# Two latent units ahead of the dilated queries, a rotation that goes through PSUM, and three neighbourhood units behind the first scores

## The reference

```python
h = rms_norm(x, g_mix[l])
proj = h @ w_in[l]
c_q, c_kv, k_r, qkv_b, qkv_c, gate_logits = jnp.split(proj, IN_SPLITS, axis=-1)
y_a = mla_mixer(c_q, c_kv, k_r, ...)            # 8 heads, latents of rank 256 and 128
q_b = apply_rope(qkv_b[:, :, 0], cos_b, sin_b)   # 12 dilated heads of 64
k_b = apply_rope(qkv_b[:, :, 1], cos_b, sin_b)
y_b = dilated_mixer(q_b, k_b, qkv_b[:, :, 2])
y_c = neighbourhood_mixer(qkv_c[:, :, 0], qkv_c[:, :, 1], qkv_c[:, :, 2], rpb[l])   # 8 heads
x = x + (gates[:, :, 0] * (y_a @ w_pa[l]) + gates[:, :, 1] * (y_b @ w_pb[l])
         + gates[:, :, 2] * (y_c @ w_pc[l])) @ w_o[l]
x = x + (silu(rms_norm(x, g_ffn[l]) @ w1[l]) * (... @ w3[l])) @ w2[l]
```

## Time and profile before

| | |
|---|---|
| median of 3 runs | 2680.39 us (2680.01 to 2680.91) |
| the profiled execution | 2676.88 us, span 2675.1 us |
| mean granted TensorE clock | 0.974 of full speed |
| TensorE matmul | 2541.6 us busy, 95 % |
| TensorE weight load | 2085.9 us, 78 % |
| GpSimd | 1975.9 us, 74 % |
| VectorE | 1182.4 us, 44 % |
| ScalarE | 688.3 us, 26 % |
| DMA | 226.62 MB, mean 85 GB/s |

### The profile page before, as it was taken

One profiled execution on the slowest core, in us unless ns is written; L12 is line 12 of the kernel. 1 busy time (PEld: TensorE's weight loads), 2 busy tenths in 40 slices (PEclk: granted clock), 3 DMA queues, 4 the chain that ended last, 5 costly groups with the idle time before them and its releaser, 6 DMA issues.

```text
span 2675.1 us, 37616 instructions
## 1 busy us (share of the span) xinstructions
PE 2541.6 (95%) x12524; PEld 2085.9 (78%) x12524; DVE 1182.4 (44%) x1608; ACT 688.3 (26%) x1299; POOL 1975.9 (74%) x1576
## 2 busy tenths in 40 slices
PE   7999999999999999999999999999998899969997
PEld 5777878777788887778788877788886778848796
DVE  6846525224312125946615223422225237550774
ACT  4435214111201013535314111210002214131341
POOL 6976763889989888976862989999897573447704
PEclk9999999999999999999999999999998899969998
DMA  3222420232232222222421232232222121102201
GB/s 130 87 95 86 151 79 27 92 98 90 95 101 94 94 95 87 79 96 86 158 79 33 86 98 91 95 101 94 94 98 86 56 80 55 41 34 86 85 11 63
DMA packets 67572, 226.62 MB, mean 85 GB/s; under 512 B 7553, under 2 KB 16257, under 8 KB 66945
## 3 DMA queue, kind: packets, MB, share of 16 engines
q1 hardware_dynamic: 66736, 223.95, 25.0%
q10 hardware_dynamic: 720, 1.17, 0.1%
HBM read 222.99 MB, written 2.10 MB: 84 GB/s over the span
## 4 chain that ended last, share of the span: by engine, by line
POOL 48%; issue 34%; PE 8%; DMA 4%; DVE 3%; POOLq 2%; SPq 0%; DVEq 0%; ACT 0%
POOL whi L460 25%; POOL wlo L463 16%; POOL raw L479 3%; POOL ada_acc L481 2%; PE ps L555 2%; PE ps L556 2%; PE ps L557 2%; DMA raw<-w_gate 1%; DMA raw<-w_abc 1%; POOLq L462 1%; POOL lnsq L487 1%; DMA raw<-w 1%; DVE q_parts L1791 1%; POOLq L105 1%; POOLq L455 0%
## 5 line engine op out<-in xcount | busy, mean ns | idle before, releaser
L460 POOL TENSOR_TENSOR whi<-raw,one 128x512 fp32r<-128x512 f32 (+3 forms) x732 | 812.9, 1111 | 563.7 <-PE ps L557 480.8
L463 POOL TENSOR_TENSOR wlo<-raw,whi 128x512 fp32r<-128x512 f32 (+3 forms) x732 | 965.3, 1319 | 57.4
L555 PE MATMUL ps<-h,whi 128*128 128x512 f32 x1984 | 793.7, 400 | 46.1 <-POOL wlo L463 19.5
L556 PE MATMUL ps<-h,whi 128*128 128x512 f32 x1984 | 777.5, 392 | 0.0
L557 PE MATMUL ps<-h,wlo 128*128 128x512 f32 x1984 | 776.6, 391 | 0.0
L555 PEld LDWEIGHTS ps<-h,whi 128*128 128x128 f32 x1984 | 374.6, 189 | 148.0 <-POOL wlo L463 34.0
L557 PEld LDWEIGHTS ps<-h,wlo 128*128 128x128 f32 x1984 | 374.4, 189 | 81.2
L556 PEld LDWEIGHTS ps<-h,whi 128*128 128x128 f32 x1984 | 375.1, 189 | 78.0 <-issue 2.4
L555 PE MATMUL ps<-y,whi 128*128 128x512 f32 x640 | 250.0, 391 | 0.6 <-DVE y L1715 0.6
L557 PE MATMUL ps<-y,wlo 128*128 128x512 f32 x640 | 249.0, 389 | 0.0
L556 PE MATMUL ps<-y,whi 128*128 128x512 f32 x640 | 249.0, 389 | 0.0
(11 more groups left out here) (253 smaller groups left out, 3232.2 us busy)
## 6 DMA issues: line engine op xcount, KB each, us to landing
raw<-w SPq DMA_DIRECT2D x120, 512.0 KB, 3.2
raw<-w_abc SPq DMA_DIRECT2D x68, 512.0 KB, 3.2
raw<-w_ada SPq DMA_DIRECT2D x48, 512.0 KB, 3.3
raw<-w_gate SPq DMA_DIRECT2D x48, 512.0 KB, 3.3
raw<-w_in SPq DMA_DIRECT2D x44, 512.0 KB, 3.3
raw<-w_pac SPq DMA_DIRECT2D x16, 512.0 KB, 3.3
raw<-w_o SPq DMA_DIRECT2D x16, 512.0 KB, 3.2
raw<-w_out SPq DMA_DIRECT2D x16, 512.0 KB, 3.3
```

What stands on the lines that cost most here:

```text
L460: pool.tensor_tensor(whi[:, s, r], raw[:, s, r], one[:, 0:1].to_broadcast([P, cols // 2]), ALU.mult).then_inc(hi_made, 1)
L463: pool.tensor_tensor(wlo[:, s, r], raw[:, s, r], whi[:, s, r].bitcast(F32), ALU.subtract).then_inc(made, 1)
L555: nc.tensor.matmul(out, whi[:, s, w], moving[:, c, :], start=(c == 0), stop=False)
L556: nc.tensor.matmul(out, whi[:, s, w], rest[:, c, :], start=False, stop=False)
```

## The change

1. The three latent units no longer stand behind the dilated tiles: units 0 and 1 of a layer are now the two c_q units, then come the twelve dilated tiles, then the c_kv unit and the rope key. The host packs the weights in this order. ScalarE reads the first latent before it takes the root for the norm and the second behind it.
2. The rotation: ScalarE makes only the four exchanged pieces and writes them to PSUM bank 4 or 5. VectorE multiplies the bank itself by the cosines (with the scale, which ScalarE gave before) into `tmp`, frees the bank, multiplies bank 4 or 5 in place by the sines, and adds the two into `qb_` or `kb_`.
3. The neighbourhood part: the third query tile's unit moves in front of the first four scores, and the fourth query tile and two key tiles follow behind them. The scores wait for the second key tile's bank, the fifth for that of the third key tile, the seventh for that of the fourth.

```diff
@@ TensorE
-                pairs(B_TILES - 1, DC, h_hi, h_lo)
-
-                for u in range(3):
-                    unit(u % 2, DC, h_hi, h_lo)
+                pairs(B_TILES, DC, h_hi, h_lo)
+                unit(0, DC, h_hi, h_lo)
                 unit(1, DC, h_hi, h_lo, m=HD)
...
-                def c_qk():
-
-                    pairs(2, DC, h_hi, h_lo)
-                    for b in range(2):
-                        pe.wait_ge(bank_free[b], free_n[b].now() + 1)
-
-                c_qk()
+                pairs(2, DC, h_hi, h_lo)
+                unit(0, DC, h_hi, h_lo)
+                pe.wait_ge(bank_free[1], free_n[1].now() + 1)
+
+                def c_qk_rest():
+
+                    for s in (1, 0, 1):
+                        unit(s, DC, h_hi, h_lo)
+
...
                 def c_scores(b, hh, bank):
+                    if b == 0 and hh in (4, 6):
+                        pe.wait_ge(bank_free[hh // 2 - 2], free_n[hh // 2 - 2].now() + 1)
...
-                          between=c_qk, ready=v_read)
+                          between=c_qk_rest, ready=v_read)
@@ ScalarE
-                            nc.scalar.activation(prob[:, s, 0:T], ps[s][:], ACT.Copy, scale=scale)
                             for half in range(4):
                                 to, frm = 32 * half, 32 * (half ^ 1)
-                                last = nc.scalar.activation(tmp[s][to:to + 32, :], ps[s][frm:frm + 32, :], ACT.Copy,
+                                last = nc.scalar.activation(ps[4 + s][to:to + 32, :], ps[s][frm:frm + 32, :], ACT.Copy,
                                                             scale=scale)
-                            last.then_inc(bank_free[s], 1)
+                            last.then_inc(swapped[s], 1)
...
+                def latent(u):
+                    act.wait_ge(unit_done[u % 2], ud_n[u % 2].next())
+                    nc.scalar.activation(c3[:, u, :], ps[u % 2][:], ACT.Copy)
+                    nc.scalar.activation(sqa[u], ps[u % 2][:], ACT.Square).then_inc(bank_free[u % 2], 1)
+
+                latent(0)
                 root(X_COLS)
+                latent(1)
...
-                for u in range(3):
-                    act.wait_ge(unit_done[u % 2], ud_n[u % 2].next())
-                    nc.scalar.activation(c3[:, u, :], ps[u % 2][:], ACT.Copy)
-                    nc.scalar.activation(sqa[u], ps[u % 2][:], ACT.Square).then_inc(bank_free[u % 2], 1)
+                latent(2)
@@ VectorE
-                            dve.wait_ge(bank_free[s], free_n[s].next())
-                            t = prob[:, s, 0:T]
-                            nc.vector.tensor_tensor(tmp[s], tmp[s], rope[:, 1, :], ALU.mult)
-                            step(nc.vector.tensor_tensor(t, t, rope[:, 0, :], ALU.mult))
+                            dve.wait_ge(swapped[s], swap_n[s].next())
+                            nc.vector.scalar_tensor_tensor(out=tmp[s], in0=ps[s][:], scalar=scale, in1=rope[:, 0, :],
+                                                           op0=ALU.mult, op1=ALU.mult).then_inc(bank_free[s], 1)
+                            nc.vector.tensor_tensor(ps[4 + s][:], ps[4 + s][:], rope[:, 1, :], ALU.mult).then_inc(half_turned, 1)
+                            dve.wait_ge(bank_free[s], free_n[s].next())
+                            dve.wait_ge(half_turned, turned_n.next())
                             to = dst[:, bass.ds(2 * j + (first + s), 1), :].rearrange("p a (f i) -> p (a i) f", f=4)
-                            nc.vector.tensor_tensor(to, t.rearrange("p (i f) -> p i f", f=4),
+                            nc.vector.tensor_tensor(to, ps[4 + s][:].rearrange("p (i f) -> p i f", f=4),
                                                     tmp[s].rearrange("p (i f) -> p i f", f=4),
                                                     ALU.add).then_inc(fin_done, 1)
```

More of the change, by code:

```diff
@@ L81 @@
 N_V2 = 48
-STEPS_1 = (2 + 3 + 2 + 2 * B_TILES + 2 + 6 + NQB * (B_HEADS + 1) + 2 + NQB + NQB * (C_HEADS + 1) + DC
+STEPS_1 = (2 + 3 + 2 + 2 + 6 + NQB * (B_HEADS + 1) + 2 + NQB + NQB * (C_HEADS + 1) + DC
            + 2 * (DC - 2) + 3)
@@ L273, in build @@
         blead_ready = sem("blead_ready")
+        swapped = [sem(f"swapped{s}") for s in range(2)]
+        half_turned = sem("half_turned")
         b_split = sem("b_split")
@@ L1382, in _ @@
             sig_n, mhi_n, mg_n, pr_n, ir_n, si_n = Count(), Count(), Count(), Count(3), Count(), Count()
+            swap_n, turned_n = [Count(), Count()], Count()
             qb_n, odd_n, mix_n, y2hi_n, qhi_n, bl_n = Count(), Count(), Count(), Count(), Count(), Count()
@@ L1491, in _ @@
             with repeat(dve, DEPTH, [(st_n, STEPS_1), (ud_n[0], UNITS_1[0]), (ud_n[1], UNITS_1[1]), (free_n[0], 55), (free_n[1], 55),
-                                     (nsum_n, 3), (std_n, 3), (rsb_n, 4), (hhi_n, 2 * DC), (post_n, 10), (rb_n, 3), (ir_n, 16),
+                                     (nsum_n, 3), (std_n, 3), (rsb_n, 4), (hhi_n, 2 * DC), (post_n, 10), (rb_n, 3), (swap_n[0], 6), (swap_n[1], 6), (turned_n, 12), (ir_n, 16),
                                      (proj_n, 8), (ch_n, 3), (bl_n, 2), (s_n, 80), (t_n, 80), (o_n, 12), (yhi_n, 12), (bias_n, 16),
@@ L1502, in _, with b_rope @@
                 nc.vector.memset(dummy[:, 13:14], 0.0)
-                def b_rope(dst, first, times):
-                    with repeat(dve, times, [(free_n[0], 1), (free_n[1], 1), (st_n, 2)]) as j:
+                def b_rope(dst, first, times, scale=1.0):
+                    with repeat(dve, times, [(free_n[0], 1), (free_n[1], 1), (swap_n[0], 1), (swap_n[1], 1),
+                                             (turned_n, 2)]) as j:
                         for s in range(2):
+                            dve.wait_ge(swapped[s], swap_n[s].next())
+                            nc.vector.scalar_tensor_tensor(out=tmp[s], in0=ps[s][:], scalar=scale, in1=rope[:, 0, :],
+                                                           op0=ALU.mult, op1=ALU.mult).then_inc(bank_free[s], 1)
+                            nc.vector.tensor_tensor(ps[4 + s][:], ps[4 + s][:], rope[:, 1, :], ALU.mult).then_inc(half_turned, 1)
                             dve.wait_ge(bank_free[s], free_n[s].next())
-                            t = prob[:, s, 0:T]
-                            nc.vector.tensor_tensor(tmp[s], tmp[s], rope[:, 1, :], ALU.mult)
-                            step(nc.vector.tensor_tensor(t, t, rope[:, 0, :], ALU.mult))
+                            dve.wait_ge(half_turned, turned_n.next())
                             to = dst[:, bass.ds(2 * j + (first + s), 1), :].rearrange("p a (f i) -> p (a i) f", f=4)
-                            nc.vector.tensor_tensor(to, t.rearrange("p (i f) -> p i f", f=4),
+                            nc.vector.tensor_tensor(to, ps[4 + s][:].rearrange("p (i f) -> p i f", f=4),
                                                     tmp[s].rearrange("p (i f) -> p i f", f=4),
@@ L1524, in b_rest @@
                     last.then_inc(b_split, 1)
-                b_rope(qb_, 0, 3)
+                free_n[0].next()
+                free_n[1].next()
+                b_rope(qb_, 0, 3, HD_SCALE)
                 b_rest(qb_, B_Q, lambda hh: (B_Q + hh, 1 - hh % 2))
@@ L1536, in _ @@
                 ud_n[0].next(8)
-                free_n[0].next(2)
+                free_n[0].next()
                 dve.wait_ge(in_tab, 16 * N_TAB)
@@ L1542, in _ @@
                                         ALU.mult).then_inc(bank_free[1], 1)
-                dve.wait_ge(bank_free[1], free_n[1].next(2))
+                dve.wait_ge(bank_free[1], free_n[1].next())
                 step(nc.vector.tensor_tensor(krt[64:96, :], krt[64:96, :], prob_3[64:96, 0:T], ALU.add))
@@ L1962 @@
     c_units = blocks(C_COL, 3 * C_TILES)
-    w_abc = np.concatenate([units(w_in, blocks(B_COL, 2 * B_TILES)), units(w_in, blocks(0, 3)), kr_unit,
+    w_abc = np.concatenate([units(w_in, blocks(0, 2) + blocks(B_COL, 2 * B_TILES) + blocks(2 * P, 1)), kr_unit,
                             units(w_in, blocks(B_COL + 2 * B_TILES * P, B_TILES) + [c_units[i] for i in (8, 9, 10, 11, 0, 1, 4, 5, 2, 3, 6, 7)])], 1)
```

## The result

The changed kernel took a median of **2660.73 us** (2656.38 to 2663.76, 4 runs) against 2680.2 us of the kernel before: ratio 0.9932, 95 % interval 0.9918 to 0.9947.

The account below looks back on a forecast made before the run. TensorE, busy 95 % of the span, was taken as the bound, so only its gaps mattered. Gains of (5.0 + 1.5 + 4.2 + 2.0) x 2 = 25.4 us gave 2655.0 us, range 2647 to 2668.

Parts of the forecast that it names:

- clock term: Half-clock stretch at the first neighbourhood scores, 370 to 375 us, taken as gone: 1.7 us a layer.
- Rotation: Dilated tiles, 40 to 125 us: 7.2 us of waits removed, 2.2 new, gain 5.0 us a layer (2.4 to 6.7).
- Splits: VectorE's splits beside GpSimd's cuts: queries 5.2 to 6.1 us, keys 4.2, with bank waits of 0.3 and 1.7 us.
- Rival 1: VectorE's splits hold the banks: rotation gains 2.4 or -0.9 us a layer, total 2660 to 2667 us; chance 0.22.
- Rival 3: Everything smooth, key split uncontended: 2651 us, or 2649 us with another clock fall spared; chance 0.12.
- Latents first: ScalarE's two operations of about 0.6 us ahead of the root: counted as nothing, 1.2 us at most without cover.
- Rope-key chain: VectorE's chain behind the rope-key unit 1.9 us shorter, TensorE waiting 1.38 us for it: gain 1.5 us a layer.
- Neighbourhood: Waits before the first scores and before the transposes: gains 2.5 and 2.0 us a layer, plus 1.7 us of clock.
- Rival 5: Wait before the first neighbourhood scores has another cause: 8.4 us missing, 2663 us; chance 0.03.
- Rival 2: Clock still falls at neighbourhood scores or newly at the key wait: two to four times 1.7 us, 2658 to 2662 us; chance 0.15.
- rival 4: ScalarE's writes into PSUM are dear: at 1.8 us a quarter copy 33 us more, 2713 us; chance 0.03.

Follow-up runs that it names:

- e6: Changed kernel with VectorE's key split behind the last two key tiles instead of ahead of them; 2652.7 us, ratio 0.9904 to the kernel before.
- e11: Changed kernel with a value unit ahead of the third dilated score's wait and both key and query splits behind all rotated tiles; 2656.2 us, ratio 0.9920.
- e2: Changed kernel with only the neighbourhood part undone, so rotation and two latent units first; 2670.7 us, ratio 0.9971 to the kernel before.
- e3: Kernel before with the neighbourhood part alone; 2664.2 us, ratio 0.9945.
- e5: The changed kernel timed again, unaltered, on a second occasion; 2654.7 us, ratio 0.9911 to the kernel before.
- e4: Kernel before with two latent units first and the old rotation through SBUF; 2677.0 us, ratio 0.9997.
- e1: Kernel before with the rotation through PSUM alone, latent and neighbourhood units where they were; 2687.1 us, ratio 1.0029.
- e8: Changed kernel with 16 of the 24 one-column matmuls moved ahead of the last latent unit; 2658.6 us, ratio 0.9921 to the kernel before.
- e9: Changed kernel with the second value unit ahead of the third dilated score's wait, latents' high parts and rests behind value tiles; 2646.2 us, ratio 0.9883.

## Why the prediction was right, and where it was off

The forecast's terms without clock, over both layers, are (5.0 + 1.5 + 2.5 + 2.0) x 2 = 22 us. Measured at full clock: 20.0 and 18.2. Its clock term was 1.7 x 2 = 3.4 us gained; measured 1.9 us *lost* on the first occasion (against the 71.9 us of the later 22 runs, and with a scatter of 2 to 3 us), and 5.2 gained on the second. That the second median lies 0.3 us from the forecast is luck: 3.8 us too little at full clock, 1.8 us more than forecast from the clock, and a kernel before that was itself 1.3 us faster that day.

*Rotation*, forecast 5.0 a layer. The fourteen units took 119.68 (the rope key's reader, of the kind of the earlier trace rows) - 40.73 = 78.95 us, forecast 78.5; before 83.6. So 4.6. The operations came as estimated: quarters 0.564 us against 0.60, multiplies 0.69, the strided add 1.12, between 0.69 and 1.65. The waits too: 0.49 (0.3) behind the query split, 1.32 (1.7) behind the key split.

*Splits.* The two in the changed kernel (VectorE's timeline):

```profile
78.62 5.39 DVE L1534 TENSOR_TENSOR y<-qb,y 64x512 fp32r<-64x512 f32 x4
...
103.70 3.84 DVE L1534 TENSOR_TENSOR y<-kb,y 64x512 fp32r<-64x512 f32 x4
```

I took 5.2 to 6.1, and 4.2. Rival 1 needed 6.1 to 7.8 for the keys and falls, though the first median lies in its range of 2660 to 2667. Rival 3, an uncontended key split of 2.8, falls by the same row. By the Trainium skill, "SBUF — State Buffer", section "Who interferes with whom", each operation with two SBUF inputs excludes a GpSimd instruction that reads SBUF; the forecast's reading of it, a full GpSimd operation waited out by each of the four, is not what the rows show. But the direction agrees: the same four pieces take 3.84 us where GpSimd cuts the half-size pieces of the rope-key unit, and 5.48 to 5.82 in e6 and e11, where it cuts full ones. The slowest single piece of the changed kernel took 1.68 us, 1.0 more than the fastest, 0.69, and one of GpSimd's operations takes 1.04 or 1.30.

*Latents first.* I counted nothing for the move itself, with ScalarE's slack as its cover, and that came out in the sum only because both parts were made together. What I did not see is the reason for the move: without it, VectorE's late tables hold the banks, 3.99 us a layer. The prediction followed a bank "in steady state" and at the two splits, never at the first tile.

*Rope-key chain*, forecast 1.5. The wait of 1.38 us is gone, but in the changed kernel nothing is gained by it: a fall of the clock behind the one-column sums takes 1.7 us of the same stretch, and the spread starts 9.74 us after the sums, where it was 9.72. Where the fall is missing, as in e2, it is 124.33 - 116.16 = 8.17 us, and the forecast's 1.5 are there. The reason was half right (VectorE's timeline):

```profile
121.09 1.55 DVE L1558 TENSOR_TENSOR krt<-krt,prob 32x512 f32<-32x512 f32 x1
122.68 0.68 DVE L1559 SCALAR_TENSOR_TENSOR krt<-krt,rsb 32x512 f32<-32x512 f32 x1
...
124.13 0.17 DVE L1574 TENSOR_SCALAR var<-var 128x8 f32<-128x8 f32 x1
...
125.42 0.17 DVE L1577 TENSOR_TENSOR rs<-rs 128x8 f32<-128x8 f32 x1
```

One of the two wide SBUF operations still meets a cut and takes 1.55 us, only another one than in the earlier trace rows. But GpSimd has no cut between 122.1 and 126.8 us, and the small operations on eight elements, of which one took 1.15 us, all take 0.17. GpSimd waits for TensorE in that time, which is at half clock for most of it. The chain ends at 125.6, 5.9 us after its start, 3.6 us before TensorE wants it; in e2, at full clock, 6.8 us after its start and 1.2 us before.

*Neighbourhood*, forecast 2.5 + 2.0 and 1.7 of clock. e3 gives 4.3 of waits a layer and 2.6 of clock. The forecast took the fall over 370 to 375 us into its sum and not the one over 397 to 402, behind the wait that it also removes: with it the clock's part is 3.4 a layer. Rival 5, by which the wait before the first scores had another cause, falls, since that wait is gone.

**The step that failed is the clock's**: "That is 0.34 x 5 = 1.7 us of TensorE work. I take it as gone", as a gain that is only ever added. It did go at that place, and a second one with it, 3.4 us over both layers that the sum left out. Rival 2 allowed for falls that stay at the neighbourhood scores or come newly at the key wait. They came at neither, but at two places that the forecast did not look at: behind the one-column sums, 3.4 us over both layers, and behind the dilated scores, 1.7 us more than before by the profile of e5 and 5.1 more by the first. Both have small matmuls in a row. So two errors of opposite sign stand in the sum, and that they nearly cancel is luck, too.

Why the clock falls behind the sums stays open. TensorE's code there is the same before and after, and it does not idle ahead of them. Counted over all profiles, that fall stands in 13 of 18 layers of the kernels that have two latents in front, with the old rotation (e4) as with the new, and in none of 6 where the three stand behind the tiles (before, e1, e3); e8, whose sums are split, is left out. But e2 has two latents in front and no such fall in either layer, so the order alone doesn't bring it.

Idle is the better supported cause at the scores. e9 took 1.74 us of it away in each layer, and a fall of 1.7 us went with it in each. At the neighbourhood scores a fall stands behind 14 of the 16 waits of 2.3 to 2.5 us in the profiles of the kernels that have them (before, e1, e2, e4), and nowhere there in the nine others. The two exceptions are both in layer 2 of e4. So such an idle often brings a fall, and not always.

ScalarE's PSUM writes (rival 4) were no dearer than its SBUF writes: 564 against 589 ns for one quarter copy (the 0.60 us of the forecast is a quarter of the span of four). The Trainium skill, "ScalarE: Activation LUTs", section "Step-by-step: what each stage is for", says that PSUM is the nearer one for ScalarE; the trace agrees, by 4 %.

## What to carry to other kernels

Where the release of a buffer is handed to another engine, follow the *first* buffer, not only the steady state: what must the new engine have done before it can touch it? A unit whose reader is another engine, put at the front, can be the whole difference between 8 us slower and 8 us faster.

Read span x clock beside the time. Its mean repeats to a microsecond or two where medians of the same kernel differ by 6, and it tells a wait that was removed from a clock that was granted. Then look where the falls are: a fall can take the place of a wait, as ahead of the spread, and hide both the gain and how little slack is left. An idle of about 2 us among small matmuls costs its own length and, in most layers here (14 of 18 and 14 of 16), 1.7 us more in clock, so the waits to remove first are those. Before a clock term goes into a forecast, count the falls at every wait that the change removes.

Before work is moved to the end of a queue, ask what chain stands behind it and how much slack it has at the *contended* duration.

## What the runs showed of the hardware

ScalarE's copy of 32x512 from PSUM to PSUM took 564 ns, to SBUF 589. VectorE's strided add of one PSUM and one SBUF operand took 1.12 us, while its multiplies with unit steps took 0.69.

The mean granted clock of a run varied from 0.968 to 0.977 over the kernels, and by up to 0.006 over the runs of one (0.970 to 0.976, kernel before). e2's eight go from 2663.2 us at 0.975 to 2676.7 us at 0.970, with span x clock between 2592.9 and 2595.3.
